# Two transformer blocks on one core: the order in which three mixers, their projections and the recurrences are woven

## The reference, cut to what matters

```
proj = h @ w_in
q_a, f_a, i_a, g_a, z_b, xbc_b, dt_b, u_c = split(proj)     # 384 384 384 384 384 896 6 256 columns
y_a = hgrn2_mixer(q_a, f_a, i_a, g_a)      # gated recurrence over chunks, 6 heads of 64
y_b = mamba2_mixer(z_b, xbc_b, dt_b)       # 4 tap convolution, silu, then chunked state space (ssd)
y_c = s5_mixer(u_c)                        # complex diagonal state space, 16 groups, then gelu and a gate
mixed = concat(y_a, y_b, y_c) @ w_out
h = layer_norm(ALPHA * h + mixed)
ff = square(relu(h @ w_mlp_in)) @ w_mlp_out
h = layer_norm(ALPHA * h + ff)
# ... the second block: gated delta rule, spatial gating, feed forward
```

## Time and profile before

| what | value |
|---|---|
| median of 3 executions | 3526.95 us |
| the profiled execution's own time | 3520.78 us |
| its span in the profile | 3519.0 us |
| TensorE busy | 3144.4 us, 89% of the span |
| VectorE, ScalarE, GpSimd busy | 1410.3, 820.8, 833.9 us |
| mean granted TensorE clock | 0.924 |

### The profile page before, as it was taken

The page is one execution under the profiler, slowest core; times in us unless marked ns, Lnnn a source line. Parts: engine busy times, 40 slices in busy tenths (PEclk is TensorE's granted clock), DMA queues, the critical chain, the costliest instruction groups (busy, mean ns, idle before and its releaser), DMA issues.

```text
span 3519.0 us, 37198 instructions
## 1 busy us (share of the span) xinstructions
PE 3144.4 (89%) x15893; PEld 2599.2 (74%) x15893; DVE 1410.3 (40%) x2146; ACT 820.8 (23%) x1071; POOL 833.9 (24%) x551
## 2 busy tenths in 40 slices
PE   8889865659899999997878989889999999999996
PEld 7768655558788888886866789866677787787784
DVE  4767265432333333336223434420104334334336
ACT  3221222210211111111236412221100322222230
POOL 0343233331211111113201145401102111111112
PEclk9999955559999999999988999999999999999998
DMA  4222211121111111111110110021020111111111
GB/s 132 53 54 77 70 36 49 31 70 68 60 48 48 48 48 48 48 48 36 64 42 25 37 43 19 13 90 54 24 108 23 38 48 48 37 47 48 48 48 72
DMA packets 156581, 180.54 MB, mean 51 GB/s; under 512 B 6320, under 2 KB 136048, under 8 KB 156416
## 3 DMA queue, kind: packets, MB, share of 16 engines
q1 hardware_dynamic: 147744, 166.51, 15.5%
q10 hardware_dynamic: 8672, 11.65, 0.9%
HBM read 158.05 MB, written 20.09 MB: 51 GB/s over the span
## 4 chain that ended last, share of the span: by engine, by line
PE 73%; DVE 10%; POOL 5%; issue 5%; ACT 3%; DMA 2%; SPq 0%; ACTq 0%; DVEq 0%; POOLq 0%
PE bank L127 72%; POOL f L158 5%; DVE f L158 4%; DVE f L166 2%; ACT f L147 2%; PE bank L142 1%; DVE f L175 1%; DVE f L163 1%; ACT r L150 1%; DMA f<-gr_s 1%; DMA f<-w_in 1%; ACT L147 1%; DVE r L158 1%; ACT f L150 0%; DMA f<-x 0%
## 5 line engine op out<-in xcount | busy, mean ns | idle before, releaser
L127 PE MATMUL bank<-r,r 128*128 128x512 f32 (+4 forms) x10824 | 2272.7, 371 | 78.5 <-DVE r L158 57.0
L127 PEld LDWEIGHTS bank<-r,r 128*128 128x128 f32 x10824 | 1880.7, 190 | 468.6 <-issue 67.1
L158 POOL TENSOR_TENSOR f<-f 128x512 f32<-128x512 f32 (+5 forms) x321 | 409.2, 1283 | 1929.7 <-ACT f L147 657.7
L158 DVE TENSOR_TENSOR f<-f,bank 128x512 f32<-128x512 f32 (+2 forms) x551 | 338.8, 638 | 462.6 <-PE bank L127 461.0
L127 PE MATMUL bank<-f 128*128 128x128 f32 (+8 forms) x2920 | 416.3, 345 | 114.3 <-DVE f L158 49.1
L127 PEld LDWEIGHTS bank<-f 128*128 128x128 f32 (+2 forms) x2920 | 359.6, 240 | 155.2 <-issue 85.7
L127 PE MATMUL bank<-f,f 128*128 128x256 f32 (+3 forms) x1556 | 412.9, 425 | 48.0 <-POOL f L158 37.5
L127 PEld LDWEIGHTS bank<-f,f 128*128 128x128 f32 (+1 forms) x1556 | 284.0, 192 | 149.6 <-issue 82.0
L158 DVE TENSOR_TENSOR r<-f,r 128x512 fp32r<-128x512 f32 (+3 forms) x137 | 186.2, 1359 | 516.7 <-ACT r L150 516.7
L166 DVE SCALAR_TENSOR_TENSOR f<-f,f 128x1024 f32<-128x1024 f32 (+2 forms) x150 | 192.7, 1285 | 391.9 <-ACT f L147 369.4
L150 ACT ACTIVATE r<-f 128x2048 fp32r<-128x2048 f32 (+3 forms) x185 | 246.5, 1352 | 405.9 <-DMA f<-w_up 182.1
(11 more groups left out here) (31 smaller groups left out, 626.8 us busy)
## 6 DMA issues: line engine op xcount, KB each, us to landing
f<-w_in SPq DMA_DIRECT2D x31, 1024.0 KB, 5.5
f<-w_up SPq DMA_DIRECT2D x44, 512.0 KB, 5.2
f<-w_mlp_in SPq DMA_DIRECT2D x16, 1024.0 KB, 5.3
f<-w_mlp_out SPq DMA_DIRECT2D x16, 1024.0 KB, 4.9
f<-w_down SPq DMA_DIRECT2D x11, 1024.0 KB, 5.0
f<-w_out SPq DMA_DIRECT2D x8, 1024.0 KB, 13.8
f<-x SPq DMA_DIRECT2D x4, 1024.0 KB, 12.0
f<-x SPq DMA_DIRECT2D x1, 4096.0 KB, 18.5
```

What stands on the lines that cost most here:

```text
L127: return self.g.matmul(out, lhs, rhs, start=start, stop=stop, skip_group_check=True)
L158: return self.g.tensor_tensor(out, a, b, op)
```

## The change

Three things change in the order of the work.

1. The pieces are ordered q, f, ig, then xb, z, dt. The first 29 (q, f, ig) run one a round, beside **two** s5 steps a round. s5 has two more empty steps ahead of its glu, 56 in all or 28 rounds.
2. hgrn follows s5 at once (`chain`, `s5_done`), and the other 30 pieces run two a round beside two hgrn steps a round. ssd follows them, two steps a round. hgrn's pair 2 and ssd wait for the end of the projections (`proj_done`).
3. Buffers move so that this fits: pairs 0 and 1 share one set of inputs (`pair_of`), pair 1's q and values are loaded when pair 0 is left; squares and outputs share storage with two factor buffers; the constant mask of the running sum goes, and one scan over 1040 columns becomes nine (16 and 8 of 128). SyncE loads panels piece by piece (`sp_proj`) instead of all ahead.

```diff
+def chain(*gens):
+    for g in gens:
+        yield from g
+
+def paced(g, first, n):
+    for _ in range(first):
+        next(g)
+        yield
+    yield from steps(g, n)
...
         P = self.pieces = []
+        for m in range(3):
+            P += [(1 + m // 2, ("q", m, h)) for h in range(2)]
+        for m in range(3):
+            P += [(1 + (3 + m) // 2, ("f", m, t)) for t in range(3)]
+        for m in range(3):
+            P += [(4 + m, ("ig", m, b)) for b in range(4)]
+            P += [(4 + m, ("ig", m, "meta"))] if m < 2 else []
+        self.first = len(P)
         for m in range(7):
-            P += [(1 + m // 2, ("xb", m, t)) for t in range(3)]
...
+            P += [(7 + m // 2, ("xb", m, t)) for t in range(3)]
+        P += [(11, ("z0", 0, b)) for b in range(4)]
+        P += [(12, ("z1", 0, b)) for b in range(4)] + [(12, ("dt", 0, "meta"))]
...
+def pair_start(k, g, i):
+    if i == 0:
+        s5_done(k, g)
+    else:
+        pair_left(k, g, i - 1)
+    if i == 2:
+        proj_done(k, g)
...
-        g.scan(G, MK, F, 0.0).then_inc(*k.up("hgrn vec", "g", i))
+        g.scan(G[:, 0:NM], k.ones[:, 0:NM], F[:, 0:NM], 0.0).then_inc(*k.up("hgrn vec", "g meta", i))
+        for c in range(8):
+            cs = slice(NM + 128 * c, NM + 128 * c + 128)
+            g.scan(G[:, cs], k.ones, F[:, cs], 0.0).then_inc(*k.up("hgrn vec", *(("g", i) if c == 7 else ("g part", i, c))))
...
-    weave(pe_s5(k, g), pe_proj(k, g))
-    weave(steps(pe_hgrn(k, g), 2), pe_ssd(k, g))
+    weave(steps(chain(padded(pe_s5(k, g), 56), pe_hgrn(k, g)), 2), paced(chain(pe_proj(k, g), pe_ssd(k, g)), k.c.first, 2))
```

More of the change, by code:

```diff
@@ L255, in steps, with padded @@
                 return
+        yield
[5 more added lines that the diff above has]
+        next(g)
+        yield
+    yield from steps(g, n)
+def padded(g, n):
+    at = 0
+    for _ in g:
+        at += 1
+        yield
+    assert at <= n, at
+    for _ in range(n - at):
         yield
@@ L506, in __init__ @@
         self.U = W.take(2 * TM).rearrange("p (c t) -> p c t", c=2)
-        self.BL = W.take(1024).rearrange("p (r c n) -> p r c n", r=2, c=4)
         self.WW = W.take(2 * 4 * TM).rearrange("p (r j t) -> p r j t", r=2, j=4)
+        W.at = W.b - 3 * (3 + TM)
+        self.below = W.at
+        self.st = [W.take(3 + TM) for _ in range(3)]
         self.CL = k.rows[:, k.late:].rearrange("p (r j n) -> p r j n", r=2, j=8)
@@ L561, in sp_c, with sp_proj @@
     g.dma(S.GLU, A["s5_glu_w"].rearrange("(k p) n -> p k n", p=128)).then_inc(*k.land("s5 in", "s5 in"))
-    for n in range(2, len(S.panels.items)):
-        S.panels.load(g, n)
+    S.panels.load(g, 2)
+def sp_proj(k, g):
+    S = k.c
+    for n, piece, third, last in S.steps():
+        if last and n + 2 < len(S.panels.items):
+            S.panels.load(g, n + 2)
+        yield
 def by_columns(k, g, w, ms, lo, hi, b):
@@ L1071, in __init__ @@
         self.an, self.ACT = sm.take(6), sm.take(128)[0:48, :]
[L1072 to L1077, removed]
+        self.XBC = [Y.take(896).rearrange("p (m t) -> p m t", m=7) for _ in range(2)]
@@ L1102, in sp_hgrn, with fetch_f @@
[L1102 to L1113, removed]
+    def fetch_f(i):
+        x = pair_of(i)
+        stored(k, g, *[("f", i, t) for t in range(3)])
+        g.dma(S.ins[x][1], dr["f_s"][i]).then_inc(*k.land(f"f in {x}", "f in", i))
@@ new lines, in fetch_g @@
+    def fetch_g(i):
+        m = 1 if i == 0 else 2
+        stored(k, g, *[("ig", m, b) for b in range(4)])
+        g.dma(S.GT[pair_of(i)].rearrange("p (c n) -> p c n", c=8), dr["ig_s"][:, 1:9, 384 + 128 * i:512 + 128 * i]).then_inc(
+            *k.land(f"gate in {pair_of(i)}", "gate in", i))
+    s5_done(k, g)
+    fetch_f(0)
+    fetch_qv(0)
+    fetch_g(0)
+    for _ in range(6):
+        yield
+    g.wait_ge(*k.past("g", 0))
+    fetch_f(1)
+    for _ in range(12):
+        yield
+    pair_left(k, g, 0)
@@ L1119, in is_level @@
+    fetch_qv(1)
+    fetch_g(1)
+    for _ in range(14):
+        yield
+    proj_done(k, g)
+    fetch_f(2)
+    fetch_qv(2)
+    fetch_g(2)
+    for _ in range(22):
+        yield
 def is_level(l):
@@ L3188, in scalar_program @@
     act_x(k, g)
-    weave(act_s5(k, g), act_proj(k, g))
-    weave(steps(act_hgrn(k, g), 2), act_ssd(k, g))
+    weave(steps(chain(padded(act_s5(k, g), 56), act_hgrn(k, g)), 2), paced(chain(act_proj(k, g), act_ssd(k, g)), k.c.first, 2))
     act_m(k, g)
@@ L3200, in vector_program @@
     dve_x(k, g)
-    weave(dve_s5(k, g), dve_proj(k, g))
-    weave(steps(dve_hgrn(k, g), 2), dve_ssd(k, g))
+    weave(steps(chain(padded(dve_s5(k, g), 56), dve_hgrn(k, g)), 2), paced(chain(dve_proj(k, g), dve_ssd(k, g)), k.c.first, 2))
     dve_m(k, g)
@@ L3213, in gpsimd_program @@
     g.wait_ge(*k.past("half"))
[L3214 to L3215 removed]
+    weave(steps(chain(padded(pool_s5(k, g), 56), pool_hgrn(k, g)), 2), paced(chain(pool_proj(k, g), pool_ssd(k, g)), k.c.first, 2))
     pool_m(k, g)
@@ L3226, in sync_program @@
     sp_c(k, g)
-    weave(steps(sp_hgrn(k, g), 2), sp_ssd(k, g))
+    weave(steps(chain(padded(iter(()), 56), sp_hgrn(k, g)), 2), paced(chain(sp_proj(k, g), sp_ssd(k, g)), k.c.first, 2))
     sp_m(k, g)
```

141 lines of the change are left out of this document (73 added, 68 removed).

## The result

| what | before | after |
|---|---|---|
| median | 3527.99 us (4 runs) | 3580.93 us (4 runs, 3574.65 to 3583.26) |
| ratio to before, 95% | | 1.0148, 1.0130 to 1.0166 |
| the profiled execution | 3520.78 us | 3581.93 us, span 3580.1 |
| glu ends | 401.9 us | 336.2 us |
| ssd ends | 778.3 us | 833.8 us |

The account below looks back on a forecast made before the run. It saw TensorE well filled beside s5 and chains between engines binding hgrn and ssd's tail; -52 - 18 + 36 + 24 + 22 gave +12 us, 3539 us against 3526.95, range 3503 to 3578.

Parts of the forecast that it names:

- B: Start of hgrn, pair 0, with two pieces a round: takes 122 us instead of 140, -18 us.
- D: hgrn's pair 2 beside two ssd steps a round: nine further steps at 2.7 us, +24 us (17 to 32).
- A: s5 alone with 29 pieces, two steps a round: glu ends at 350 us instead of 401.9, -52 us.
- by VectorE's rotations and not by the pieces: In s5, what sets the time from y to y of a tile, taken as 31.3 and 31.6 us.
- 7.6 us: In pair 0, from a tile's last piece through VectorE's taps to the next factors, partly covered by TensorE.
- Woven pieces keep the clock up: In pair 0's rounds 32 to 35: a level takes 1.84 us instead of 3.68 at the half clock.
- C: hgrn's pair 1, rounds 38 to 46, with pieces and ssd's preamble: 147 us instead of 111, +36 us.
- E: ssd's tail after hgrn: 12 steps remain instead of six, at 3.6 us each, +22 us.
- 2.7, the middle: Price in us of a further ssd step beside hgrn, between its TensorE time 1.9 and the tail's pace 3.6.
- Rival 2: Pieces cover the waits in rounds 29 to 46, which stay under 35 us: -30, 3509 us; chance 0.29.
- Rival 3: Each table switch between silu and hgrn's exponentials is waited for: 17 us more, 3556, to 3580 with coarser queues; chance 0.21.
- Rival 4: The clock stays at its lower level in woven rounds, doubling about 190 us of TensorE work: over 3600; chance 0.03.

Follow-up runs that it names:

- run 4: The changed kernel with VectorE's convolution taps and ScalarE's silu and store two pieces later in their queues, nothing left out: 3557.51 us, 1.0091 to the kernel before.
- run 2: The changed kernel with a convolution tile's three taps replaced by one single-column operation: 3550.46 us, 1.0069 to the kernel before.
- run 9: The changed kernel with taps and silu two pieces later and ssd's chunk loads issued earlier: 3539.73 us, 1.0043 to the kernel before.
- run 1: The changed kernel with ssd making one step a round instead of two, projections still two pieces a round: 3572.86 us, 1.0131 to the kernel before.
- run 10: The changed kernel with later taps and silu, earlier chunk loads, and ssd one step a round: 3539.29 us, 1.0034 to the kernel before.
- run 7: The changed kernel with only ssd's chunk loads earlier, each waiting for readers of the buffer it overwrites: 3562.27 us, 1.0108 to the kernel before.
- the tie: Against the kernel before: new piece order, hgrn right after s5, but one s5 step, piece and ssd step a round: 3512.24 us; with earlier chunk loads 3500.79 us.

## Why the prediction was wrong

The direction was right, and so was its ground, that the rounds which take the pieces over give back more than s5 gains. The size was not: +53, outside the range. Two steps failed above all: B's price of the taps, which took the waits short and the clock as kept (22 us), and D's price of a further ssd step, which left out the wait for chunk data (17 us).

- **A, -52 forecast, -66 measured.** Pauses and the low clock came as said. Mis-sized was the step "by VectorE's rotations and not by the pieces", 31.5 us from y to y: it took 27.4, since a panel's split, which is the pieces' work, stood among the rotations before and stands there no more. The 23.3 us ahead of y(1,0) held one too and became 18.7. That is 4.6 of what is missing in the second tile: the sum puts y(1,0) 105 us after y(0,1) (195 to 300, which is 332 less 31.6), and it was 98.7.
- **B, -18 forecast, +4 measured.** The step that failed is "7.6 us, of which TensorE covers 1.8 where the tile ends the round (5.7 idle, once), 5.9 where it ends the round's first piece (1.6, twice)". The 5.7 was right (5.2); the two of 1.6 were 5.5 and 3.9, as the 7.6 us left out the panels, which stood ahead of the taps once and beside them once. Larger still was what the step put at nothing: behind each of the three waits the clock was down, 1.7 us on a score and 1.6 on the round's two pieces, 10 us in all, where the longer waits are 5.7 (14.6 in sum for 8.9). "Woven pieces keep the clock up" was true only where the waits were short: the granted clock was 0.80 in pair 0, 1.00 in pair 1's levels (541 to 598 us), whose one wait is 1.47 us. The other 6 us lie in the rounds at the pair's two ends. With the taps moved back, pair 0 takes 124 us, for a forecast of 122. That the place of the taps, with the silu behind them, costs 22 us in all is shown by run 4; how it divides between wait and clock is read from rows and was not tried by itself.
- **C, +36 forecast, +53 measured.** The levels fit: rounds 41 to 44 took 57 us for 58. Rounds 38 and 39 took 41 us for 38: TensorE idles 22.2 us ahead of the kd transposes, and the pieces behind it go at the lower clock, 9.3 us for 7.97. Round 40 took 20 for 16, with the panel wait at 6.7 us for 5, and round 46 took 17 for 14. The step that failed most is round 45, 29 us for 21: "2.9 for that", from the last store to ssd's preamble. The preamble opens with a memset in GpSimd's queue, behind an operation of hgrn's output that waits for VectorE, and so starts 8 us after the last piece. Leaving out the taps took 7 us off this stage (run 2), moving them none or 3 (166 us in run 4, 161 in run 9), and one ssd step a round 10 (run 1) or 6 (run 10). The rest of its miss has had no experiment of its own.
- **D and E, +46 forecast, +65 measured.** "Since the two steps stand behind each other in each queue but share the round with hgrn" left out SyncE's queue: no term priced the chunk loads, although the profile of before has 17.5 us of waits for them. They cost 17 us (run 7), 8 in pair 2 and 9 in the tail by the windows of run 9. With them hidden, pair 2 takes 135 us and the tail 38, for 128 and 43. The price of a further step, "2.7, the middle", was too low, since the steps shared nothing with hgrn: 4.4 us with the late loads (run 1 against the change), above both bounds, and 3.3 with them hidden (run 10 against run 9), near the upper one.
- **Rival 2** (the pieces cover the waits) fell: it needed waits under 35 us in rounds 29 to 46. TensorE is idle for 86 us from 336 to 644 us, of which 18.9 and 22.2 stand ahead of the kd transposes.
- **Rival 3** had a time nearer to the result (3556, and 3580 with coarse queues), but its named mechanism is refuted: 16 table loads fewer save 3 to 6 us, not 17 to 20. Here they are nearly free; ScalarE was busy for 54 of the 144 us of pair 0. The Trainium skill (ScalarE: Activation LUTs, "Table sets: the hidden batching unit") says to batch activations by table set, and its section "What ACT_TABLE_LOAD costs" puts a switch at about 2.66 us, a load and a drain. The trace shows the load alone, 1.28 us, with activations right ahead of it and right behind it. What held of the rival is its second sentence, that queues of coarser steps wait longer, and the lines are VectorE's and SyncE's.
- **Rival 4** had a part: the clock did fall in woven rounds, though behind waits, and not for good.

That run 9 lands at 3539.73 us, the forecast's number, is partly chance: A's 14 us too many and C's 14 too few cancel there.

By parts, then: the tie is worth -13 us and -26 with early loads; the weave of pieces into hgrn and of two steps a round turns that into +53. The taps' place is 22 of it. The chunk loads are 17, but early loads give some 12 in the tie as well, so only some 5 are the weave's. Some 40 us more against the tie remain with both mended (+15 against -26), and they are not ssd's second step, which costs nothing there (run 10). What is left is the pace of s5 and of the pieces: s5's 66 us gained do not pay for 30 pieces in rounds whose waits are chains across ScalarE and VectorE. That is read from the stages; no run took these 40 us apart, nor the buffers that move with the pace.

## What to carry to other kernels

Before work is woven into a stage that is bound by a chain, list for each queue what will stand ahead of the chain's next link: a 4 us operation ahead of a 1.3 us one cost 5 us of wait, and then 3 us more by the lower clock on the score and the pieces behind it. Put the woven work behind the link, and let each load wait for the one buffer that it overwrites. And time the parts of a change alone: here the sum is 53 us slower, and one part of it, with earlier loads, is 26 us faster.

## What the runs showed of the hardware

That TensorE can slow after a single short wait in an otherwise busy stretch: after the wait of 5.53 us the next score took 3.68 us and the round's pieces 9.58 instead of 7.97; in run 9 the score behind a wait of 1.67 us took 2.95 us. So a wait can cost more than its length, but its length alone does not tell: in run 2 the score behind 1.73 us took 2.00 us, the full clock's, and the one behind 1.42 us took 3.06. That VectorE slows beside GpSimd's panel split: 7.1 and 8.2 us for three taps instead of 4.0, 20.6 and 20.7 us for 16 rotations instead of 16.3. And taking away 34 us of TensorE's waits for one releaser gave only 17 us, as the releasers behind it were late by the other half.
